# Second block: first convolution in three fp32r passes with low parts on GpSimd, and a new order of taps, inversion, z tiles and gate tiles

## The chip, the cores and the metric

One NeuronCore of a Trainium2 chip runs the whole program in one launch. The metric is the device time in microseconds of one execution; the inputs lie in device memory when it starts. TensorE is PE in the profile, VectorE is DVE, ScalarE is ACT, GpSimd is POOL, and SyncE (SP) issues most DMAs.

## The reference

All values are float32. The reference runs two networks, one behind the other, on 256 tokens of width 1024. The first (two layers of attention with Fourier mixing) fills the first 2058 us and is not touched. The second block is touched, in its mixer:

```python
hn = rmsnorm(h_res, norm_mix_g) * (1.0 + sc1) + sh1
proj = hn @ w_in        # a_qkv, a_z, a_gates, b_qk, b_v, b_o, b_gates, merge
a_qkv = silu(centred_conv(a_qkv, gdn_conv_w))      # 1536 channels, five taps along the tokens
aq, ak, av = split(a_qkv, 3)                        # q and k are normalised per head
o_a = gated delta rule of (aq, ak, av, g, beta), both directions, in chunks of 64
o_a = rmsnorm(o_a, gdn_norm_g) * silu(a_z)
b_qk = silu(centred_conv(b_qk, mlstm_conv_w))      # 1024 channels, five taps
h_b = mLSTM of (bq, bk, b_v, gates), both directions, in chunks of 64
h_b = head_layernorm(h_b) * sigmoid(b_o)
y = sigmoid(merge_a) * (o_a @ w_branch_a) + sigmoid(merge_b) * (h_b @ w_branch_b)
h_res = h_res + gt1 * (y @ w_out)
```

In each chunk the delta rule solves a unit lower triangular system of 64 rows. After the mixer comes a mixture of 32 experts (two per token, chosen in one of four groups), whose weights are some 100 MB, and a last norm.

## The kernel before

Activations lie transposed: a tile has 128 channels on the partitions and 256 tokens along the free axis. A projection tile is eight matmuls (k = 0 to 7, 128 rows of weights each) into one of seven PSUM banks, which a ring gives out in order of use. Engines run lists of instructions written out by hand (`pe_second`, `act_second`, `dve_second`, `pool_second`); there is no scheduler. An engine executes its list in order, and `e.wait_ge(*at(...))` waits for a named event of another engine, or of its own. Python generators mix two lists in fixed turns: each `yield` is a place at which the other list may get a turn.

A matmul of two fp32 operands takes several passes inside the array. The other form, `products` with `three` (L353), splits each operand into a high part (a copy to the fp32r type, by ACT) and a low part (the operand less the high part, by DVE, L539 and L1976) and makes three fp32r matmuls: high x low, low x high, high x high.

The second mixer, in the order of PE:

1. Norm of the input into U (eight tiles, L1080 on DVE, L1067 on ACT), then two gate tiles (L2259).
2. Twelve tiles of the first convolution ("gdn": four of k, four of q, four of v), fp32 x fp32 (L2038). For each, ACT copies the bank into one of three padded tiles `xp` (L2058), DVE multiplies by the first tap (L2065) and adds four more taps (L2070). ACT takes SiLU and squares of pairs of tiles (L2081, L2087). After the sixth tile PE makes the head sums (L2097) and turns k to tokens (L554), for which it waits for the squares of the first four tiles. The last two tiles are mixed into step 3.
3. Blocks: for each of eight heads, decays (L2156, L2143) and products of k with k (L2340), exponentials on ACT (L2352), 32x32 blocks on DVE (L2365).
4. Chunks: for each head, two decays and four products (L2433, L2434) in three banks, eight exponentials on ACT, two multiplications on DVE (L2447). The four z tiles (`pe_tile`, L2664) stand behind heads 1 to 4. DVE mixes in the inversion of the 32x32 blocks (`dve_invert`, L2381 and L2386: 62 short dependent steps, then two transposes, L2388 and L2389), the last convolution tile, and four right-hand sides (`dve_rhs`, L2466). The inverse is then copied into place (L2403 on ACT, L2411 on DVE).
5. Four tiles of the second convolution ("mlstm"), then the solve (`pe_solve`, L2477, L2488, L2504, L2509), with four more tiles of that convolution as filler.
6. The scan over chunks (L2607, L2622) beside the projections of v and the output gate (L2687, L2664) and DVE's gate rows of the mLSTM (`dve_gates_b`).
7. `pe_gdn_out`: the output of four pairs of heads, each with its norm. The "gate b" tiles, in three passes, are mixed in (`pe_gate_b`, L545): tile 0 ahead of the wait for the scan, tile f+1 in turn f, tiles 5 to 7 in the mLSTM loop (`pe_mlstm`) at heads 1, 3 and 5. Their high parts are made by ACT (L1970), their low parts by DVE (L1976).
8. The mLSTM, the "gate a" tiles and branches, the output projection, the router and the experts. The SP queue issues the experts' loads (L3651) in a fixed order, each when its place is free; before the first it waits for the last output of the mLSTM.

Weights come in loads of 2 MB into four slots `wr`. `late_low` names the same memory as the slots with the fp32r type: a low part takes the place of its raw weights. POOL has little to do in this block: two memsets for the unit matrix (L2574, L2576), one of the inverse's place (L2578), and at the end the indirect loads of some experts.

## Time and profile before

| | us |
|---|---|
| median of 3 runs | 2684.06 |
| lowest, highest | 2683.41, 2684.50 |
| profiled execution | 2682.79 |
| its span | 2681.0 |
| PE, DVE, ACT, POOL busy | 2600.6, 1634.2, 1002.4, 66.9 |
| granted TensorE clock, mean | 0.988 |

The span runs from the first to the last instruction of the profiled execution. Busy shares are averages over stages with different limits, so the stretches below are to be read one by one. The profile's matmul of fp32 operands is recorded as two instructions. A wait is put down to the event that came last.

### The profile page before, as it was taken

The numbers are of one execution on the slowest core, as the hardware profiler recorded it, in microseconds if no ns is written. First come the engines' busy times: TensorE is split into PE (matmuls) and PEld (weight loads), VectorE is DVE, ScalarE is ACT, GpSimd is POOL, SyncE is SP. The second block draws the span as 40 slices with busy tenths as digits, with TensorE's granted clock in tenths as the row PEclk, the third lists the DMA queues.
The fourth block names the chain that finished last, engine by engine and source line by source line (L and its number), as shares of the span: only waits on it lengthen the run. The fifth ranks groups of instructions, "written<-read, shape, count | busy, mean of one in ns | idle before, by whom it ended". The sixth has DMA issues, their size and how long they took to land.

```text
span 2681.0 us, 37410 instructions
## 1 busy us (share of the span) xinstructions
PE 2600.6 (97%) x15326; PEld 2148.8 (80%) x15326; DVE 1634.2 (61%) x2906; ACT 1002.4 (37%) x1777; POOL 66.9 (2%) x91
## 2 busy tenths in 40 slices
PE   8999999999999999999999999998999999999896
PEld 5888888867889888888888898798999787886453
DVE  4867766366446877648767465765555777675221
ACT  5322233266434322234222243664444442543121
POOL 0000000000000000000000000000000000000320
PEclk9999999999999999999999999999999999999998
DMA  7535442200222445434467433134345202149997
GB/s 320 198 155 225 179 182 95 95 32 32 77 112 95 175 178 220 165 126 157 174 250 281 158 123 132 43 134 181 139 180 192 95 32 95 64 172 418 412 395 322
DMA packets 48841, 456.55 MB, mean 170 GB/s; under 512 B 10784, under 2 KB 11168, under 8 KB 13344
## 3 DMA queue, kind: packets, MB, share of 16 engines
q1 hardware_dynamic: 41472, 446.01, 42.9%
q0 software_dynamic: 6912, 6.32, 0.7%
q8 instruction: 122, 2.00, 0.3%
q10 hardware_dynamic: 288, 1.84, 0.2%
q14 instruction: 47, 0.39, 0.0%
HBM read 497.11 MB, written 1.05 MB: 186 GB/s over the span
## 4 chain that ended last, share of the span: by engine, by line
PE 86%; DVE 7%; ACT 3%; DMA 3%; issue 2%; SPq 0%; POOL 0%; ACTq 0%; DVEq 0%; POOLq 0%
PE ps L545 68%; PE ps L3917 2%; PE ps L2038 2%; PE ps L1427 1%; PE ps L1450 1%; DMA BIG<-edn 1%; PE ps L554 1%; DMA BIG<-eup,extra_ids 1%; PE ps L3943 1%; PE nb L3943 1%; ACT fh L532 1%; DMA wr<-ws 1%; PE ps L3957 1%; PE ps L2664 1%; DVE fl L539 1%
## 5 line engine op out<-in xcount | busy, mean ns | idle before, releaser
L539 DVE TENSOR_TENSOR fl<-wr,fh 128x1024 fp32r<-128x1024 f32 (+2 forms) x436 | 481.9, 1107 | 446.0 <-ACT fh L532 445.2
L545 PE MATMUL ps<-UL,fh 128*128 128x512 f32 (+1 forms) x2096 | 731.9, 349 | 11.5 <-DVE UL L894 5.3
L545 PE MATMUL ps<-UH,fl 128*128 128x512 f32 (+1 forms) x2096 | 729.5, 348 | 0.0
L545 PE MATMUL ps<-UH,fh 128*128 128x512 f32 (+1 forms) x2096 | 729.1, 348 | 0.0
L532 ACT CAST fh<-wr 128x1024 fp32r<-128x1024 f32 (+2 forms) x436 | 414.4, 954 | 321.0 <-PE ps L545 298.8
L545 PEld LDWEIGHTS ps<-UL,fh 128*128 128x128 f32 x2096 | 397.7, 190 | 65.5 <-DVE UL L894 6.0
L545 PEld LDWEIGHTS ps<-UH,fh 128*128 128x128 f32 x2096 | 397.9, 190 | 49.8
L545 PEld LDWEIGHTS ps<-UH,fl 128*128 128x128 f32 x2096 | 397.7, 190 | 49.5
L597 DVE SCALAR_TENSOR_TENSOR acc<-wr,CA 128x1024 f32<-128x1024 f32 x256 | 312.4, 1220 | 3.7
L545 PE MATMUL ps<-HL,fh 128*128 128x512 f32 (+1 forms) x770 | 267.4, 347 | 0.0
L545 PE MATMUL ps<-HH,fl 128*128 128x512 f32 (+1 forms) x770 | 266.9, 347 | 0.0
L545 PE MATMUL ps<-HH,fh 128*128 128x512 f32 (+1 forms) x770 | 266.9, 347 | 0.0
L1247 ACT CAST HH<-rot 128x512 fp32r<-128x512 f32 (+1 forms) x88 | 50.0, 568 | 344.0 <-DVE rot L1290 344.0
L545 PEld LDWEIGHTS ps<-HL,fh 128*128 128x128 f32 x770 | 145.8, 189 | 18.3
L545 PEld LDWEIGHTS ps<-HH,fl 128*128 128x128 f32 x770 | 145.8, 189 | 18.1
L545 PEld LDWEIGHTS ps<-HH,fh 128*128 128x128 f32 x770 | 145.8, 189 | 18.0
L1290 DVE TENSOR_TENSOR rot<-ps,rot 128x512 f32<-128x512 f32 (+1 forms) x88 | 54.9, 623 | 137.7 <-PE ps L545 137.7
L1241 ACT ACTIVATE rot<-ps 128x512 f32<-128x512 f32 (+1 forms) x88 | 47.9, 545 | 203.3 <-PE ps L545 203.0
L3917 PE MATMUL ps<-wr,BIG 128*32 128x512 f32 x344 | 78.6, 613 | 1.5 <-DMA wr<-eup,extra_ids 1.5
L2038 PE MATMUL ps<-U,wr 128*128 128x256 f32 x320 | 74.0, 386 | 0.0
L3917 PE MATMUL ps<-BIG 128*32 128x512 f32 x284 | 71.4, 615 | 0.1
L2038 PEld LDWEIGHTS ps<-U,wr 128*128 128x128 f32 x320 | 60.4, 193 | 8.8 <-issue 0.4
(624 smaller groups left out, 3833.2 us busy)
## 6 DMA issues: line engine op xcount, KB each, us to landing
wr<-ws SPq DMA_DIRECT2D x135, 2048.0 KB, 8.1
wr<-ws SPq DMA_DIRECT2D x32, 1408.0 KB, 6.1
wr<-eup SPq DMA_DIRECT2D x27, 1024.0 KB, 17.3
BIG<-eup SPq DMA_DIRECT2D x26, 1024.0 KB, 14.2
wr<-edn SPq DMA_DIRECT2D x12, 1024.0 KB, 11.2
wr<-ws SPq DMA_DIRECT2D x11, 1024.0 KB, 6.9
BIG<-edn SPq DMA_DIRECT2D x11, 1024.0 KB, 10.0
X<-eup SPq DMA_DIRECT2D x6, 1024.0 KB, 11.6
```

Source lines behind the costliest of these rows:

```text
L532: e.copy(sp.tiles(n)[0], raw_tile(sp.units[n])).then_inc(*hi_done.inc("high", event))
L539: e.tensor_tensor(lv, raw_tile(sp.units[n]), hv.bitcast(F32), ALU.subtract).then_inc(*low_done.inc("low", event))
L545: i = e.matmul(out, l, r, start=first and n == 0, stop=last and n == len(pairs) - 1, skip_group_check=True)
L554: return e.transpose(out, in_, CC[0:k, 0:k])
L597: e.scalar_tensor_tensor(out=ACC[:, :], in0=w[:, q, :], scalar=1.0, in1=cb_rows[c], op0=ALU.mult, op1=ALU.mult, accum_out=to).then_inc(*mo ...
L1241: e.activation(s[:, 0:T], psum.of("gated", name, half, p, 0)[:, 0:T], ACT.Silu).then_inc(*act.inc("gated", name, half, p, 0))
L1247: e.copy(HH[:, p, 0:T], s[:, 0:T]).then_inc(*act.inc("h high", name, half, p))
L1290: e.tensor_tensor(s[:, 0:T], psum.of("gated", name, half, p, 1)[:, 0:T], s[:, 0:T], ALU.mult).then_inc(*dve.inc("gated", name, half, p, 1))
L1427: e.matmul(b[:, 0:khi - klo], qT[64 * c:64 * c + 64, h, q0:q0 + 128], kT[64 * c:64 * c + 64, h, klo:khi], start=True, stop=True, skip_grou ...
L2038: i = e.matmul(b[:, 0:256], w[:, k, q * 128:q * 128 + 128], U[:, k, 0:256], start=k == 0, stop=k == 7, skip_group_check=True)
L3917: i = e.matmul(b[o:o + 32, :], XG[(p // 2) % 2][:, k, 128 * (p % 2) + o:128 * (p % 2) + o + 32], up_weights(n, h, k % 4), start=k == 0, st ...
L3943: i = e.matmul(b[o:o + 32, :], actT[p % 2][:, q, o:o + 32], down_weights(n, q, h), start=q == 0, stop=q == 1, skip_group_check=True)
```

## The change

- The twelve tiles of the first convolution are made in three fp32r passes. ACT makes a high and DVE a low part of U (`act_conv_u`, `dve_conv_u`: two instructions of 128x1024 each). ACT makes the high part of each weight tile, in four rotating sets; POOL makes the low parts (`pool_conv_lows`), ahead of its memsets.
- In both convolutions ACT applies the middle tap while it reads the PSUM bank (a second instruction beside its copy), and DVE adds the other four. The first of DVE's five instructions goes.
- Inversion: its steps are spread over DVE's list 2, 4, 2, 7 to a place where they were 2 and, late, 5; the last two of the four early right-hand sides move into `dve_solve`.
- z tiles: behind heads 1, 3, 5 and 7; ACT copies them at heads 2, 4 and 6 and after the loop.
- Gate tiles: "gate b" tiles 0 and 1 stand ahead of the wait for the scan, tile f+2 in turn f, tiles 6 and 7 at heads 1 and 3 of the mLSTM. DVE makes the end blocks of the mLSTM in turn 1 of `dve_gdn_out`.

```diff
@@ -378,6 +378,7 @@
 
         columns_in = tally("columns_in")
         router_in = tally("router_in")
+        pool_low = tally("pool_low_parts")
         ident_in = tally("ident_in")
         x_in = tally("x_in")
         rope_in = tally("rope_in")
@@ -1863,6 +1864,7 @@
         ktok = big(1024, 2, 512)
         vtok = big(2048, 2, 1024)
         zf = big(1024, 4, 256)
+        intra_at = off[0]
         intra = big(4096, 8, 512)
         cross_at = off[0]
         CROSS = big(4096, 8, 512)
@@ -1975,6 +1977,38 @@
             e.wait_ge(*at("high", u))
             e.tensor_tensor(l, late_tile(weights(late_load(u)), u), h.bitcast(F32), ALU.subtract).then_inc(*low_done.inc("low", u))
 
+        CUH, CUL = [over(n, 4096 + cross_at + 2048 * i, [128, 8, 256]) for i, n in enumerate(("CUH", "CUL"))]
+        conv_sets = [over(f"ch{i}", 4096 + intra_at + 1024 * i, [128, 1024]) for i in range(4)]
+
+        def conv_parts(n):
+            n, load, q, wn, dst = conv_tiles("gdn")[n]
+            cols = slice(128 * q, 128 * q + 128)
+            raw, low = [t.rearrange("p (k n) -> p k n", k=8)[:, :, cols] for t in (weights(load), late_low[slot_of[load]][:, :])]
+            return load, raw, conv_sets[n % 4][:, :].rearrange("p (k n) -> p k n", k=8), low
+
+        def act_conv_high(e, n):
+            load, raw, high, low = conv_parts(n)
+            e.wait_ge(*at("loaded", load))
+            if n >= 4:
+                e.wait_ge(*at("conv proj", "gdn", n - 4))
+            e.copy(high, raw).then_inc(*hi_done.inc("high", "conv", n))
+
+        def pool_conv_lows(e):
+            for n in range(12):
+                load, raw, high, low = conv_parts(n)
+                e.wait_ge(*at("high", "conv", n))
+                e.tensor_tensor(low, raw, high.bitcast(F32), ALU.subtract).then_inc(*pool_low.inc("low", "conv", n))
+
+        def act_conv_u(e):
+            for i in range(2):
+                e.copy(CUH[:, 4 * i:4 * i + 4, :], U[:, 4 * i:4 * i + 4, 0:256]).then_inc(*act.inc("conv u high", i))
+
+        def dve_conv_u(e):
+            for i in range(2):
+                s = slice(4 * i, 4 * i + 4)
+                e.wait_ge(*at("conv u high", i))
+                e.tensor_tensor(CUL[:, s, :], U[:, s, 0:256], CUH[:, s, :].bitcast(F32), ALU.subtract).then_inc(*dve.inc("conv u", i))
+
         def act_late_u(e):
             e.wait_ge(*at("slot free", ("win2", 2080, 512)))
             for i in range(2):
@@ -2032,11 +2066,19 @@
             b, old = psum.take("conv in", tag, n)
             if old:
                 e.wait_ge(*at(*old))
-            if q == 0:
+            if tag == "gdn":
+                load, raw, high, low = conv_parts(n)
+                if n == 0:
+                    e.wait_ge(*at("conv u", 1))
+                e.wait_ge(*at("low", "conv", n))
+            elif q == 0:
                 e.wait_ge(*at("loaded", load))
             for k in range(8):
-                i = e.matmul(b[:, 0:256], w[:, k, q * 128:q * 128 + 128], U[:, k, 0:256], start=k == 0, stop=k == 7,
-                             skip_group_check=True)
+                if tag == "gdn":
+                    i = products(e, b[:, 0:256], three(high[:, k, :], low[:, k, :], CUH[:, k, :], CUL[:, k, :]), k == 0, k == 7)
+                else:
+                    i = e.matmul(b[:, 0:256], w[:, k, q * 128:q * 128 + 128], U[:, k, 0:256], start=k == 0, stop=k == 7,
+                                 skip_group_check=True)
                 if k % 2 and k < 7:
                     yield
             i.then_inc(*sums.inc("conv proj", tag, n))
@@ -2055,18 +2097,22 @@
             if (tag, n) == ("gdn", 0):
                 e.wait_ge(*at("conv edges"))
             e.wait_ge(*at("conv proj", tag, n))
-            e.copy(xp[:, 2:258], psum.of("conv in", tag, n)[:, 0:256]).then_inc(*act.inc("conv in", tag, n))
+            n, load, q, wn, dst = conv_tiles(tag)[n]
+            b = psum.of("conv in", tag, n)
+            e.copy(xp[:, 2:258], b[:, 0:256]).then_inc(*act.inc())
+            e.activation(dst, b[:, 0:256], ACT.Identity, scale=col("cva" if tag == "gdn" else "cvb", wn * 5 + 2, 1)).then_inc(
+                *act.inc("conv in", tag, n))
 
         def dve_conv(e, tag, n):
             n, load, q, wn, dst = conv_tiles(tag)[n]
             ck = "cva" if tag == "gdn" else "cvb"
             xp = xps.of("conv taps", tag, n)
             e.wait_ge(*at("conv in", tag, n))
-            e.tensor_scalar(dst, xp[:, 0:256], col(ck, wn * 5, 1), None, ALU.mult).then_inc(*dve.inc())
-            for i in range(1, 5):
-                before = dve.now()
-                yield
-                e.wait_ge(*before)
+            for i in (0, 1, 3, 4):
+                if i:
+                    before = dve.now()
+                    yield
+                    e.wait_ge(*before)
                 e.scalar_tensor_tensor(out=dst, in0=xp[:, i:i + 256], scalar=col(ck, wn * 5 + i, 1), in1=dst,
                                        op0=ALU.mult, op1=ALU.add).then_inc(*dve.inc())
             dve.mark("conv taps", tag, n)
@@ -2553,6 +2599,7 @@
                                      *[itertools.chain(dve_conv(e, "mlstm", n), dve_first_block_out(e, col("fin"), n - 4))
                                        for n in range(4, 8)])
             for n in range(2):
+                dve_rhs(e, 2 + n)
                 for _ in dve_conv(e, "mlstm", n):
                     pass
             for n in range(8):
@@ -2877,8 +2924,8 @@
                 pe_chunks(e, h)
                 if h == 6:
                     pe_to_tokens(e, "v a", zf, ("conv silu", 11))
-                if 1 <= h <= 4:
-                    pe_tile(e, "z", h - 1, ("win2", 1536, 512), h - 1, h == 4)
+                if h % 2:
+                    pe_tile(e, "z", h // 2, ("win2", 1536, 512), h // 2, h == 7)
             for n in range(4):
                 pe_conv(e, "mlstm", n)
             pe_solve(e)
@@ -2889,6 +2936,9 @@
 
         def act_second(e, prev):
             act_norm_pair(e, "nmix", prev, m2[:, 0])
+            act_conv_u(e)
+            for n in range(2):
+                act_conv_high(e, n)
             act_log_exp(e)
             e.activation(st[0:64, 8:9], a_log, ACT.Exp).then_inc(*act.inc("a log"))
             act_softplus(e, "a", NX)
@@ -2896,8 +2946,10 @@
             for to, src in ((NEGR, CA[:, 0:256]), (CROSSR, CA[:, 256:512]), (ROWR, CA[:, 512:576]), (IDR, ident)):
                 e.copy(to[:, :], src).then_inc(*act.inc())
             act.mark("consts2 parts")
+            act_conv_high(e, 2)
             for n in range(9):
                 act_conv(e, "gdn", n)
+                act_conv_high(e, n + 3)
                 if n == 8:
                     e.wait_ge(*at("C"))
                     act_row_high(e, "B", RHB, BC)
@@ -2927,17 +2979,21 @@
                     act_row_high(e, "E", RHE, EA)
                 if h in (2, 5):
                     act_conv(e, "gdn", 10 + (h - 2) // 3)
+            def act_z(q):
+                e.wait_ge(*at("z proj", q))
+                e.copy(z_raw[:, q, :], psum.of("z", q)[:, 0:256]).then_inc(*act.inc("z", q))
+
             for h in range(8):
                 act_chunks(e, h)
                 if h == 6:
                     act_to_tokens(e, "v a", vtok)
-                if 2 <= h <= 5:
-                    e.wait_ge(*at("z proj", h - 2))
-                    e.copy(z_raw[:, h - 2, :], psum.of("z", h - 2)[:, 0:256]).then_inc(*act.inc("z", h - 2))
+                if h in (2, 4, 6):
+                    act_z(h // 2 - 1)
                 if h == 3:
                     for n in (8, 10):
                         act_silu_square(e, n)
                     act_log_exp(e)
+            act_z(3)
             e.wait_ge(*at("products sum", 7))
             e.wait_ge(*act.now())
             e.activation(zs, z_raw, ACT.Silu).then_inc(*act.inc("z open"))
@@ -2965,6 +3021,8 @@
             e.memset(eps64, 64 * EPS).then_inc(*dve.inc())
             dve.mark("conv edges")
             dve_norm_pair(e, "nmix", col("fin"), col("nmix"), m2[:, 1])
+            e.wait_ge(*at("u", "nmix", 7))
+            dve_conv_u(e)
             gates = dve_gdn_gates(e)
             next(gates)
             e.wait_ge(*at("gate sum", 1))
@@ -2989,7 +3047,7 @@
                 dve_blocks(e, h)
                 if h == 1:
                     dve_end_blocks(e, "gdn", ends)
-                for _ in range((0, 0, 0, 0, 1, 1, 1, 2)[h]):
+                for _ in range((0, 0, 0, 0, 1, 1, 1, 1)[h]):
                     next(taps)
                 if h == 4:
                     dve_row_low(e, "A", RHA, AR)
@@ -3000,7 +3058,7 @@
                                            op1=ALU.add).then_inc(*dve.inc("A"))
             invert = dve_invert(e)
             for n, _ in enumerate(dve_beside(e)):
-                for _ in range(2 if n < 14 else 5):
+                for _ in range(2 if n < 5 or 7 <= n < 11 else 4 if n < 7 else 7):
                     next(invert, None)
             for _ in invert:
                 pass
@@ -3024,12 +3082,13 @@
                 if h == 1:
                     yield from dve_conv(e, "gdn", 11)
             e.wait_ge(*at("tokens", "v a", 1))
-            for h in range(4):
+            for h in range(2):
                 dve_rhs(e, h)
                 yield
 
         def pe_gdn_out(e):
             pe_gate_b(e, 0)
+            pe_gate_b(e, 1)
             e.wait_ge(*at("scan a"))
             for f in range(4):
                 b, old = psum.take("o square", f)
@@ -3052,7 +3111,7 @@
                             i = e.matmul(b[pp, 64 * n:64 * n + 64], SP[pp, s, o:o + 64], qg[pp, 2 * f + dr, 64 * n:64 * n + 64],
                                          start=False, stop=True, skip_group_check=True)
                 i.then_inc(*sums.inc("o", f))
-                pe_gate_b(e, f + 1)
+                pe_gate_b(e, f + 2)
                 b, old = psum.take("o root", f)
                 if old:
                     e.wait_ge(*at(*old))
@@ -3065,6 +3124,7 @@
 
         def act_gdn_out(e):
             act_gate_b(e, 0)
+            act_gate_b(e, 1)
             for f in range(4):
                 r, old = heads_rot.take("gdn out", f)
                 if old:
@@ -3077,7 +3137,7 @@
                 e.activation(r[:, 256:512], psum.of("o root", f)[:, 0:256], ACT.Ln, scale=1.0 / 64, bias=eps[:, :]).then_inc(*act.inc())
                 e.wait_ge(*act.now())
                 e.activation(r[:, 256:512], r[:, 256:512], ACT.Exp, scale=-0.5).then_inc(*act.inc("o root", f))
-                act_gate_b(e, f + 1)
+                act_gate_b(e, f + 2)
                 act_late_high(e, 4 + f)
                 if f:
                     act_oa_high(e, f - 1)
@@ -3097,6 +3157,8 @@
                     e.wait_ge(*at("z open"))
                 e.tensor_tensor(oaT[:, f, :], oaT[:, f, :], zs[:, f, :], ALU.mult).then_inc(*dve.inc("gdn out", f))
                 dve_late_low(e, 3 + f)
+                if f == 1:
+                    dve_end_blocks(e, "mlstm", MP[:, 20:24])
                 if f > 1:
                     dve_oa_low(e, f - 2)
 
@@ -3126,8 +3188,8 @@
                     tk = slice(tt * 128, tt * 128 + 128)
                     i = e.matmul(b[:, tk], kb[pp, f, tk], qb[pp, f, tk], start=True, stop=True, skip_group_check=True)
                 i.then_inc(*sums.inc("kq", "mlstm", h))
-                if h in (1, 3, 5):
-                    pe_gate_b(e, 5 + h // 2)
+                if h in (1, 3):
+                    pe_gate_b(e, 6 + h // 2)
             for s in range(3):
                 for dr in range(2):
                     n, tt, pb = chunk_of(s, dr)
@@ -3221,8 +3283,8 @@
                         e.activation(r[:, o:o + 128], b[:, o:o + 128], ACT.Exp,
                                      bias=CTB[:, tt, 0, 32 * dr + h:32 * dr + h + 1]).then_inc(*act.inc())
                 act.mark("exp decay", "mlstm", h)
-                if h in (1, 3, 5):
-                    act_gate_b(e, 5 + h // 2)
+                if h in (1, 3):
+                    act_gate_b(e, 6 + h // 2)
                 if h % 2:
                     act_late_high(e, 8 + h // 2)
             e.wait_ge(*act.now())
@@ -3282,7 +3344,6 @@
             dve_late_low(e, 7)
             dve_oa_low(e, 2)
             dve_oa_low(e, 3)
-            dve_end_blocks(e, "mlstm", MP[:, 20:24])
             e.wait_ge(*at("cols", "mlstm", 1))
             for _ in dve_pairs(e, "qi", qg, qb):
                 pass
@@ -4181,6 +4242,7 @@
         def _(e):
             for l in range(2):
                 pool_mirror(e, l)
+            pool_conv_lows(e)
             pool_second(e)
             pool_expert_loads(e)
```

## Rows read from the trace of the kernel before

**Rows 1.** Busy by stretch: us, PE, PEld, DVE, ACT, POOL (counts), clock, DMA share, GB/s
```profile
2070.50:2109.50 39.00, 38.23 (x181) 32.27 (x180) 27.07 (x67) 15.79 (x27) 0.00 (x0) 1.00 0.43 162
2109.50:2131.00 21.50, 20.94 (x109) 16.57 (x110) 15.57 (x41) 13.27 (x44) 0.00 (x0) 1.00 0.18 59
2131.00:2188.50 57.50, 51.15 (x249) 43.32 (x247) 46.66 (x114) 29.88 (x82) 3.51 (x1) 0.91 0.14 52
...
2304.00:2330.00 26.00, 26.00 (x181) 23.13 (x182) 14.69 (x25) 15.46 (x41) 0.00 (x0) 0.87 0.21 81
...
2391.00:2681.00 290.00, 253.60 (x1974) 144.68 (x1974) 93.04 (x239) 66.68 (x135) 48.05 (x48) 0.96 0.96 389
```

**Rows 2.** Timeline of SP's queue, first expert load: start, us, engine, line, operation
```profile
2391.84 0.45 SPq L3651 DMA_DIRECT2D wr<-eup  x1
```

**Rows 3.** Chain of waits: start, us, what; six tiles now, then three-pass products
```profile
2070.65 20.73 PE ps L2038 x96
...
2379.42 4.31 PE ps L545 x36
```

**Rows 4.** Timeline of ACT, a copy of a tile and a high part of weights
```profile
2091.46 0.37 ACT L2058 COPY BIG<-ps 128x256 f32<-128x256 f32 x1 [3.08 <-PE ps L2038]
...
2283.23 1.05 ACT L1970 CAST lh<-wr 128x1024 fp32r<-128x1024 f32 x1
```

**Rows 5.** Timeline of DVE: first tap, four taps, a low part of weights
```profile
2091.87 0.35 DVE L2065 TENSOR_SCALAR BIG<-BIG,K 128x256 f32<-128x256 f32 x1 [1.02 <-ACT BIG L2058]
2092.26 2.04 DVE L2070 SCALAR_TENSOR_TENSOR BIG<-BIG,K 128x256 f32<-128x256 f32 x4
...
2283.97 1.22 DVE L1976 TENSOR_TENSOR late<-wr,lh 128x1024 fp32r<-128x1024 f32 x1
```

**Rows 6.** Timeline of POOL: copy and subtraction alone, then one beside DVE
```profile
573.05 0.19 POOL L1726 COPY acc<-rot 128x2 f32<-128x2 f32 x1 [8.91 <-ACT rot L1666]
573.19 0.45 POOL L1727 TENSOR_TENSOR acc<-rot 128x127 f32<-128x127 f32 x1
...
629.39 0.91 POOL L1727 TENSOR_TENSOR CA<-rot 128x127 f32<-128x127 f32 x1
```

**Rows 7.** Timeline of DVE at the same place
```profile
629.31 1.55 DVE L1798 TENSOR_TENSOR FL<-acc,FH 128x512 fp32r<-128x512 f32 x2
630.78 0.94 DVE L1798 TENSOR_TENSOR FL<-RS,FH 128x512 fp32r<-128x512 f32 x1
631.85 0.69 DVE L1798 TENSOR_TENSOR FL<-CA,FH 128x512 fp32r<-128x512 f32 x1
```

**Rows 8.** Timeline of DVE in the chunks, a wait
```profile
2159.89 0.69 DVE L2447 TENSOR_TENSOR BIG<-ps,BIG 128x512 f32<-128x512 f32 x1 [3.78 <-ACT BIG L2352]
```

**Rows 9.** Timeline of PE: mLSTM tiles, first and second products of the solve
```profile
2170.40 14.08 PE L2038 MATMUL ps<-U,wr 128*128 128x256 f32 x64
2188.57 1.63 PE L2477 MATMUL ps<-acc,BIG 128*128 128x128 f32 x8 [4.09 <-issue]
...
2192.94 1.05 PE L2477 MATMUL ps<-acc,BIG 128*128 128x128 f32 x8
```

**Rows 10.** Timeline of ACT, the inverse copied into place
```profile
2182.85 3.29 ACT L2403 COPY BIG<-BIG 32x512 f32<-32x512 f32 x3 [1.35 <-DVE BIG L2388]
```

**Rows 11.** Timeline of PE, outputs of the first two pairs of heads
```profile
2274.37 1.98 PE L3042 MATMUL ps<-BIG 128*64 128x128 f32 x16 [2.16 <-DVE BIG L2835]
...
2282.05 1.09 PE L3042 MATMUL ps<-BIG 128*64 128x128 f32 x16
```

**Rows 12.** Timeline of ACT, root of a norm in pe_gdn_out's second turn
```profile
2287.52 0.47 ACT L3077 ACTIVATE rot<-ps,eps 128x256 f32<-128x256 f32 x1 [2.51 <-PE ps L3060]
```

**Rows 13.** Timeline of DVE: second turn, first wait of the mLSTM loop, its last low part
```profile
2288.48 0.48 DVE L3093 SCALAR_TENSOR_TENSOR BIG<-BIG,K,rot 128x256 f32<-128x256 f32 x1 [3.29 <-ACT rot L3079]
...
2315.12 0.69 DVE L3296 TENSOR_TENSOR BIG<-ps,rot 128x512 f32<-128x512 f32 x1 [4.99 <-PE ps L3127]
...
2328.41 1.21 DVE L1976 TENSOR_TENSOR late<-wr,lh 128x1024 fp32r<-128x1024 f32 x1
```

## Prediction

> **What bounds the kernel now.** I read the stages first, as busy time by stretch [rows 1]: from 2070.5 us on, PE is busy 38.23 of 39.00 us while twelve convolution tiles begin, then 20.94 of 21.50, then 51.15 of 57.50. Over the last 290 us the DMA engines are 0.96 busy: the experts' weights set the end there. Their first issue is at 2391.84 us [rows 2], and it stands behind the last mLSTM output. So what the second block gains or loses before 2391.84 moves the whole DMA-bound tail with it, microsecond for microsecond, and none of it is hidden. The question is when the last mLSTM output comes. Then I followed the chain of waits and, where it names PE, asked who is next behind. I take four stretches, A to D.
>
> **A: the twelve tiles in three passes (2070.5 to 2131 us).** Six tiles of four-pass fp32 take 20.73 us, 3.455 each; 36 fp32r passes of the same width take 4.31, so 24 take 2.87 [rows 3]. PE saves 12 x 0.58 = 7.0 us.
>
> The price is on three engines. ACT makes 12 high parts at 1.05 and 12 first taps about as long as its 0.37 copy [rows 4]: 17 us more beside its 15.79 + 13.27 of 60.5 [rows 1], bearable, but in series with its copies. DVE gains: a tile's first tap (0.35) goes, 2.04 for four taps stays [rows 5]; it pays two low parts of U, 1.22 each [rows 5]. POOL makes 12 low parts. The trace has no such instruction of 1024 elements. A 128x127 one took 0.45 and a 128x2 copy 0.19 [rows 6]: (0.45 - 0.19) x 1024/127 + 0.19 = 2.3 us. Scaling the whole 0.45 gives 3.6; from below stands DVE's 1.22 for the same subtraction [rows 5]. I take 2.3, worked out on its own engine, and under PE's 2.9: POOL alone doesn't pace the tiles.
>
> What decides is POOL beside DVE. At 629.39 us the 0.45 us instruction took 0.91, while DVE ran subtractions with both inputs in SBUF [rows 6]. DVE's three took 2.41 (629.31 to 631.72) where one alone takes 0.69 [rows 7]: at least 0.34 lost to the two POOL reads of 0.26 each. POOL's extra 0.46 is more than its own reading time of 0.26 (0.45 less the 0.19 of start), which two engines sharing each cycle fairly couldn't make of it; waiting for a whole DVE instruction can. So I read an exclusive turn per instruction, and four taps (all with two SBUF inputs) meet it. DVE then loses some 2.1 us per low part, less 0.1 of start-up: 2.04 + 2.0 = 4.05 us per tile, against 3.455 now. That row is one of 127 elements; that it holds through a 2.3 us instruction is my extrapolation.
>
> What the row can't show, the length of the turn for long instructions, the Trainium skill states, and it speaks against this change ("SBUF — State Buffer", section Who interferes with whom): a VectorE instruction with two SBUF inputs and a GpSimd one that reads SBUF exclude each other, and the later one is blocked until the first has finished, however long that is. By this rule a low part of any length blocks DVE for all of it and the sum is the forecast's; by the row taken alone (turns no longer than 0.26 us shown) it would be rival 1's.
>
> Stepping it through: the U parts end on ACT at 2069.2 and on DVE at 2070.6; the first low part is there at 2072.8, so PE starts 2.2 us late and, as after its 2.16 us gap in [rows 11], runs slow for some 3 us, at the lower of the two clocks, 1.2 GHz (1.5 lost). ACT issues high part n+3 as soon as copy n is out, which may be up to three tiles ahead of DVE (three xp buffers), so POOL runs to low part 8 while DVE is at tile 3. By the time that tile 3 has its taps, DVE and POOL have spent 9 x 2.1 = 19 us of POOL's reading, 4 x 2.04 = 8.2 of taps and some 4 of gate rows (busy 27.07 in the stretch [rows 1], less nine tiles of 2.4 and the row parts), in the 31.4 us since 2070.6: the turns are the bound. Tile 3 ends near 2102; the squares, the head sums and the tokens of k wait for it, and PE takes tile 6 at about 2105, 10 us later than now. After that come tiles 6 to 8, three low parts (6.3), gate rows and tap work of 10, less what PE's shorter tiles give. DVE starts its blocks 14 us later; the blocks themselves shift whole. A = +14. The two memsets of the unit matrix now stand behind the low parts on POOL's queue, near 2120; the inversion that waits for them starts at 2135 or later, so they cost nothing, and lose this cover only if POOL runs 15 us over. The loads that wait for the slots of these tiles come later by as much as the tiles; DMA is 0.43 and 0.18 busy there [rows 1], and no wait for them is due. Bounds: with low parts of 1.22 us the count gives 12 x 1.1 less, +1; if the turns cost nothing, ACT's longer series leaves +1.5 (PE's 7.0 are eaten by the late start, the clock, and ACT's squares and table loads between longer tiles); with 3.6 us low parts the same count gives 12 x 1.3 = 16 more, +30.
>
> **B: inversion, chunks, z tiles (2131 to 2188.5).** DVE waits 3.78 us, and 3.2 once more, for products held up behind z tiles [rows 8]. With a z tile after every second chunk and the inversion's 62 steps packed 4 and 7 to a place, they end right behind chunk 7, before the right-hand sides, of which two move behind the inversion. DVE is through its copies some 8 us earlier. But PE stands behind: its four mLSTM tiles run 14.08 us from 2170.40 and end at 2184.5, and the solve starts at 2188.57 after 4.09 idle [rows 9]. Only that gap can go. ACT's third mLSTM copy still waits for its tile (PE at 2181.1, three of the four), and 3.29 us of inverse copies follow it [rows 10], so the solve starts near 2185.3: -3.3. The gap also cost clock: the first eight products took 1.63 against 1.05 afterwards [rows 9], 0.6, and the tile steps behind them, twice the work, some 1.3 (an estimate from that). B = -5.2, between -2 (DVE's longer chunk spacing stalls PE) and -8.
>
> **C: solve.** The two moved right-hand sides lie in DVE's wait for the first cross products; a first tap less per tile shortens its end. -0.5, between +1 and -1.5.
>
> **D: gates (2274 to 2330).** Gate tile 1 goes ahead of the wait for the scan, where PE idles 2.16 us and then runs slow (1.98 against 1.09 for the same sixteen) [rows 11]. The cost: tile f+2 now needs the low part that DVE makes in turn f-1. From PE's norm: 0.96 to DVE's start (ACT from 2287.52, DVE from 2288.48), 0.48 and a second like it (0.4), then 1.22 = 3.1 us [rows 5, 12, 13]; PE has only the outputs of 1.9 to do meanwhile, so 1.2 us of stall in each of three turns, +4 at the last norm. In the mLSTM loop, PE then has two gate tiles where it had three, and DVE, which waited 4.99 us there for PE, becomes the pace: loop and low parts end near 2325.6 in place of 2329.6 [rows 13]. The end blocks' instruction moves under a wait, worth nothing more. D = -4.0, between 0 (the stalls bring the lower clock) and -6.
>
> **Sum.** +14 - 5.2 - 0.5 - 4.0 = +4.3 on the profiled execution's own 2682.79 us (span 2681.0 and 1.8 around it) is 2687.1; the median of the runs is 1.3 above that execution, so 2688.4.
>
> **Rivals.**
> 1. *POOL's reads don't hold DVE up* (the 629 us row was something else, or a long instruction lets DVE in between). For it: only short instructions were seen. Against: both engines' lengthenings there match. A = +1.5 to +5; total 1.5 - 9.7 = -8 to -5: 2676 to 2679. DVE's taps stay near 0.51 apart.
> 2. *Lock and lower clock together*, the slower side: PE's gaps of 7 us in A and of 1.2 us in D each bring the clock of 1.2 GHz, as the gap of 4.09 did [rows 9]. Three drops at 1.7 us beyond those counted, and D at 0: +4.3 + 5 + 4 = +13, 2697. It decides once PE waits over about 2 us at three more places. For: stretch 2304 to 2330 is at 0.87 already [rows 1]. Against: DVE, not PE, would be the bound in A, and hides PE's slowness there.
> 3. *Low parts as slow as 3.6 us*: total +20, 2704. Against it: the fixed 0.19 is seen in the copy.
>
> **How the numbers follow.** A comparison of this kernel can tell about 0.2%, 5.4 us, from no change. Lock as forecast: 0.56, spread 4 to each side: same 0.34, slower 0.20, faster 0.02. Rival 1: 0.34, faster 0.30, same 0.04. Rivals 2 and 3: 0.10, slower. Together faster 0.32, same 0.38, slower 0.30. Likeliest's own range 2683 to 2694; with both sides 2674 to 2698.
>
> **What would show it.** Right: DVE's tap instructions in A with many of 2 us and more, beginning beside POOL subtractions; POOL's at 2.2 to 2.5; tile 6 on PE at about 2105; PE idle 15 us in all between 2070 and 2125; the solve without a gap before it; three waits of PE for the low parts of gates; first expert issue near 2396. Wrong: taps at 0.48 throughout, and tiles on PE 2.9 apart (rival 1); granted clock under 0.9 in A and D (rival 2). If POOL's instruction is shorter than 1.9 us, A falls by 12 x 0.4 and the sum to zero.

## The result

The changed kernel takes 2700.56 us in the median of six runs (2694.63 to 2704.63), against 2683.90 for six of the kernel before; the ratio is 1.006 [1.005, 1.0069]. The forecast was 2688.4 with 2674 to 2698: the direction was right, the size was not. The profiled execution took 2703.9 us (span 2702.1, granted clock 0.984); it is the second slowest of the six.

I read both traces at the same six places and take differences of differences, so what the first block leaves as run-to-run offset drops out (the second block's first U part is at 2061.94 in the trace of before and at 2065.05 after; nothing ahead of it was changed).

| stretch, by its last event | forecast | measured |
|---|---|---|
| A: to DVE's first inversion transpose | +14 | +18.0 |
| B: to the start of the solve on PE | -3.3 (and -1.9 of clock behind it) | -2.7 |
| C, and D to ACT's last norm | -0.5 + 4 | +6.4 |
| D: mLSTM loop, to DVE's memset | -8 | -3.5 |
| tail, to the first expert load | 0 | 0.0 |

With the +3.1 of offset the sum is the +21.3 of the first expert load, which answers to [rows 2]:

```profile
2413.13 0.44 SPq L3712 DMA_DIRECT2D wr<-eup  x1
```

Busy time by stretch of the changed kernel (time, PE, PEld, DVE, ACT, POOL, granted clock, DMA share, GB/s), beside [rows 1]: in the first, PE is busy 25.88 of 39.00 us where it was busy 38.23, at a granted clock of 0.82 where it was 1.00; POOL is new with 21.84; no engine is full. The last row is the mLSTM loop.

```profile
2073.60:2112.60 39.00, 25.88 (x177) 23.82 (x177) 30.45 (x42) 21.31 (x37) 21.84 (x9) 0.82 0.28 108
2112.60:2155.00 42.40, 32.86 (x217) 28.36 (x215) 32.31 (x64) 26.05 (x68) 10.77 (x6) 0.96 0.27 100
2155.00:2207.00 52.00, 50.30 (x244) 42.75 (x243) 47.38 (x114) 29.96 (x81) 1.21 (x1) 0.90 0.11 41
2323.07:2351.07 28.00, 26.41 (x183) 22.90 (x182) 19.11 (x32) 18.87 (x50) 0.00 (x0) 0.88 0.20 76
```

POOL's low parts in the same trace (start, us, engine, line): all twelve take 2.34 to 2.70 us, 2.44 in the median, where 2.3 was forecast, but with idle time between them that ends with ACT's high part. Three of the rows:

```profile
2079.05 2.38 POOL L2000 TENSOR_TENSOR late<-wr,ch 128x1024 fp32r<-128x1024 f32 x1 [0.63 <-ACT ch L1994]
2097.44 4.64 POOL L2000 TENSOR_TENSOR late<-wr,ch 128x1024 fp32r<-128x1024 f32 x2 [3.77 <-ACT ch L1994]
2115.69 2.40 POOL L2000 TENSOR_TENSOR late<-wr,ch 128x1024 fp32r<-128x1024 f32 x1 [13.61 <-ACT ch L1994]
```

DVE there. Four taps take 2.04 where POOL stands still (2095.07 to 2097.11) and 4.18 or 6.19 beside it; eight scans take 5.93, where they took 1.68 before (the same line then L2242). A blocked instruction is longer by up to 2.2 us, most of a low part: the chain of waits has single taps of 0.50 and of 2.63, and the gate row of L2270 takes 2.63 for 0.42 (before: L2224).

```profile
2081.51 4.18 DVE L2116 SCALAR_TENSOR_TENSOR BIG<-BIG,K 128x256 f32<-128x256 f32 x4 [4.43 <-ACT BIG L2103]
2085.61 2.63 DVE L2270 SCALAR_TENSOR_TENSOR BIG<-BIG 128x256 f32<-128x256 f32 x1
2088.28 6.19 DVE L2116 SCALAR_TENSOR_TENSOR BIG<-BIG,K 128x256 f32<-128x256 f32 x4
2095.07 2.04 DVE L2116 SCALAR_TENSOR_TENSOR BIG<-BIG,K 128x256 f32<-128x256 f32 x4
2097.15 5.93 DVE L2288 TENSOR_TENSOR_SCAN BIG<-BIG 32x64 f32<-32x64 f32 x8
2103.49 5.96 DVE L2116 SCALAR_TENSOR_TENSOR BIG<-BIG,K 128x256 f32<-128x256 f32 x12
```

PE's waits in the changed kernel, where they matter: the late start, the long gap ahead of the head sums, and behind it tile 6 (A); the solve's start, a gap inside it and its last products (B, C); low parts of gate tiles (D).

```profile
2076.04 0.36 PE L546 MATMUL ps<-CUL,ch 128*128 128x256 f32 x1 [2.28 <-POOL late L2000]
2106.92 1.97 PE L2143 MATMUL ps<-rot,CA 128*64 128x256 f32 x4 [9.94 <-ACT rot L2133]
2110.44 0.56 PE L546 MATMUL ps<-CUL,ch 128*128 128x256 f32 x1
2206.97 1.16 PE L2523 MATMUL ps<-acc,BIG 128*128 128x128 f32 x8 [0.60 <-ACT BIG L2449]
2244.07 1.97 PE L2550 MATMUL ps<-acc,BIG 128*128 128x64 f32 x16 [1.73 <-DVE acc L2608]
2250.93 1.91 PE L2555 MATMUL ps<-BIG,rot 128*64 128x128 f32 x16
2298.80 0.36 PE L546 MATMUL ps<-UGL,lh 128*128 128x256 f32 x1 [1.49 <-DVE late L1978]
2305.97 0.36 PE L546 MATMUL ps<-UGL,lh 128*128 128x256 f32 x1 [1.35 <-DVE late L1978]
```

### The profile page after: what moved, and what is told of

Same layout as the page of the kernel before. It is cut to its first block, busy times and chain, and to the rows that moved or that the text cites. A ratio compares the mean times of both kernels' runs of the same rounds, so it can differ in the third digit from the quotient of the medians.

```text
span 2702.1 us, 37648 instructions
## 1 busy us (share of the span) xinstructions
PE 2602.7 (96%) x15422; PEld 2151.9 (80%) x15422; DVE 1649.4 (61%) x2888; ACT 1022.8 (38%) x1811; POOL 96.5 (4%) x103
## 3 DMA queue, kind: packets, MB, share of 16 engines
q8 instruction: 123, 2.02, 0.3%
## 4 chain that ended last, share of the span: by engine, by line
PE 83%; DVE 8%; ACT 4%; DMA 3%; issue 2%; POOL 0%; SPq 0%; ACTq 0%; DVEq 0%; POOLq 0%
PE ps L546 68%; PE ps L3978 2%; PE ps L1451 1%; PE ps L1428 1%; DMA BIG<-edn 1%; PE ps L555 1%; DVE BIG L2116 1%; ACT fh L533 1%; DMA BIG<-eup 1%; PE ps L4004 1%; DMA wr<-eup,extra_ids 1%; PE ps L4018 1%; DVE fl L540 1%; PE nb L4004 1%; PE ps L2734 1%
## 5 line engine op out<-in xcount | busy, mean ns | idle before, releaser
L1242 ACT ACTIVATE rot<-ps 128x512 f32<-128x512 f32 (+1 forms) x88 | 47.9, 545 | 203.3 <-PE ps L546 203.0
L1615 ACT ACTIVATE BIG<-ps,st 128x512 f32<-128x512 f32 (+1 forms) x96 | 58.0, 620 | 21.4 <-DVE st L1785 21.2
L1785 DVE TENSOR_REDUCE st<-ps 128x1 f32<-128x512 f32 (+1 forms) x96 | 50.9, 592 | 24.2 <-PE ps L1428 24.2
```

What stands on the lines that cost most here:

```text
L1242: e.activation(s[:, 0:T], psum.of("gated", name, half, p, 0)[:, 0:T], ACT.Silu).then_inc(*act.inc("gated", name, half, p, 0))
L1615: e.activation(dst[:, 0:nk], psum.of("p", l, n, qb, c)[:, 0:nk], ACT.Exp, bias=st[:, z + c:z + 1 + c], scale=-1.0, accum_out=st[:, z + 4 + ...
L1785: e.tensor_reduce(st[:, z + c:z + c + 1], psum.of("p", l, n, qb, c)[:, 0:nk], AX.X, ALU.min).then_inc(*dve.inc("least", l, n, qb, c))
```

## The experiments

The theory was the forecast's: POOL's subtractions and DVE's instructions with two SBUF inputs take turns at SBUF, each for a whole instruction. Rivals for A were a longer series on ACT, the late start, and sharing by bytes; for D, the lower clock against the waits for low parts. The stretches below are differences from the trace of before, as in the table above (A | B | C and D to the last norm | loop):

| kernel | median us | ratio | A | B | C, D | loop |
|---|---|---|---|---|---|---|
| changed | 2700.6 | 1.0060 [1.0050, 1.0069] | +18.0 | -2.7 | +6.4 | -3.5 |
| split_only | 2701.9 | 1.0067 [1.0053, 1.0081] | +19.3 | -1.0 | -0.3 | 0.0 |
| no_split | 2681.2 | 0.9994 [0.9984, 1.0005] | +0.3 | -2.8 | +4.8 | -6.5 |
| dve_lows | 2684.3 | 1.0001 [0.9992, 1.0010] | +8.6 | -3.0 | +4.8 | -4.2 |
| pool_memset | 2684.4 | 1.0000 [0.9991, 1.0009] | -1.8 | -2.9 | +4.8 | -4.1 |
| pool_copy | 2683.6 | 0.9990 [0.9981, 1.0000] | +3.2 | -2.6 | +6.4 | -3.5 |
| pool_eighths | 2690.8 | 1.0025 [1.0014, 1.0036] | +15.5 | -3.2 | +4.8 | -4.2 |
| eighths_apart | 2692.8 | 1.0029 [1.0018, 1.0040] | +10.8 | -2.9 | +4.7 | -4.1 |
| inv_taps | 2685.1 | 1.0003 [0.9994, 1.0012] | +0.4 | -2.9 | +0.3 | +1.5 |
| gates_only | 2685.2 | 1.0004 [0.9995, 1.0013] | 0.0 | -0.1 | +4.4 | -3.5 |
| early_lows | 2677.2 | 0.9978 [0.9969, 0.9987] | +0.4 | -2.8 | +0.6 | -4.2 |
| early_four | 2676.5 | 0.9968 [0.9956, 0.9980] | +0.3 | -2.8 | -1.4 | -2.7 |
| early_four_gate6 | 2674.8 | 0.9967 [0.9955, 0.9979] | +0.4 | -2.9 | -1.4 | -6.9 |

A profile is one execution; the medians are over 5 to 11, and one kernel's runs lie up to 13 us apart (no_split: 2677.2 at a mean clock of 0.989 to 2690.1 at 0.986). Stretches are what I compare; totals only where the intervals part. A stretch stands for its one execution, and that isn't always a typical one: the profile of dve_lows (2688.1) is the slowest of its eleven runs, that of pool_memset (2678.9) the fastest of its eleven, that of pool_eighths (2696.4) the slowest of its seven. So dve_lows and pool_memset lie 10.4 us apart in A and 0.1 us apart in the median.

**Which part costs.** split_only is the kernel before with the three-pass tiles alone.

```diff
+            pool_conv_lows(e)        # and the tiles in three passes, U parts, high parts
             pool_second(e)           # taps, inversion, z tiles, gates: as before
```

> The kernel before with only the three-pass tiles (U parts, high parts by ACT, low parts by GpSimd); taps, inversion, z tiles and gates as before. Theory (GpSimd subtractions and DVE instructions with two SBUF inputs take exclusive turns, one instruction at a time): the tiles cost about what the changed kernel shows in that stretch, +17 us, so 2698 to 2704, with taps of 4.18 us for two beside the subtractions. Rival (the stretch is long because the changed taps and ACT's longer series hold it up, not the parts): under +8 us, below 2692. Rival (the other three edits together gain nothing): equal to the changed kernel, 2700.6.

It came out at 2701.93, with the taps lengthened as in the changed kernel (0.77 us in the mean). That is the theory's range and also the last rival's number: the total alone can't tell them apart. no_split is the reverse.

```diff
-                    i = products(e, b[:, 0:256], three(high[:, k, :], low[:, k, :], ...
+                    i = e.matmul(b[:, 0:256], w[:, k, q * 128:q * 128 + 128], U[:, k, 0:256], ...
```

> The changed kernel without its three-pass tiles: fp32 tiles in four passes again, no parts of U and none of the weights; the taps, the inversion, the z tiles and the gates as changed. Theory (from the stretches of the changed kernel: B -2.7, C +1.1, D +0.9 with the stalls of 1.2 us in the gates): -1 to -3 us against before, 2681 to 2683. My forecast's terms B, C and D (-5.2, -0.5, -4.0) would give -9.7, 2674. Rival (the stalls and the losses in C and D come from GpSimd's late work or from the shifted loads of the three-pass tiles): -6 us or more, below 2678.

2681.22, in the theory's range: the three passes cost 19 us, all of the loss and more, and the rest, forecast at -9.7, gives 3.3, with an interval that holds no change.

**What of the three passes costs.** dve_lows moves the twelve low parts to DVE, pool_memset takes POOL's reads away, pool_copy leaves it one input.

```diff
-            pool_conv_lows(e)
+                dve_conv_low(e, n + 3)      # dve_lows: behind the taps of tile n
---
-                e.tensor_tensor(low, raw, high.bitcast(F32), ALU.subtract)...
+                e.memset(low.bitcast(F32), 0.0)...      # pool_memset, twice
+                e.tensor_copy(low, raw)...              # pool_copy
```

> The changed kernel, but the twelve low parts are made by DVE (1.2 us each, 14.6 us more of DVE work) and GpSimd makes none. Theory of exclusive turns: DVE gets back about 12 x 2.1 us of blocked time and pays 12 x 1.2, so the first stretch costs some 8 us less than in the changed kernel: 2689 to 2694. Rival (no exclusion; the two engines share, so work moved onto the busier DVE costs its full 14.6 us, less what GpSimd's late parts cost PE): not under 2700, up to 2710.

> The changed kernel, but in place of each low part of the first convolution's weights GpSimd sets the same 1024 columns to zero, twice: the low parts are left out of the products, all instructions of the other engines stay. GpSimd is about as busy and writes more, but it reads nothing. Theory (its reads are what shuts DVE out): DVE's taps at 0.5 us, the first stretch at +2 to +5 instead of +17: 2685 to 2690. Rival (GpSimd's writes or its semaphores hold DVE up as well): taps stay above 1 us each and the time above 2697.

> The changed kernel, but GpSimd copies the weight's 1024 columns in place of subtracting (one input from SBUF instead of two; the low parts are left out of the products, a copy stands in their place). If any GpSimd read takes the port for its whole instruction, DVE's taps beside it last 1 us and more, in step with the copy's length (about 1.2 to 1.5 us), and the first stretch costs +5 to +12: 2689 to 2697. If only GpSimd instructions with two inputs do, the taps stay at 0.48 and the time is that of the memsets, 2684.

dve_lows gives DVE 12 x 1.22 us more to do and still ends A 9.4 us sooner; its median, 16 us below the changed kernel's, is better than the 2689 to 2694 that I expected. In pool_memset all the other instructions stand, POOL is busy 2 x 0.954 per tile (a low part took 2.44), and A is 19.8 us shorter than in the changed kernel: at -1.8, and 2684.4 in the median, it lies under the +2 to +5 and the 2685 to 2690 that I expected. Its groups in 2068 to 2130, DVE's taps and scans, POOL's memsets, and one more of DVE's (last: busy, mean ns):

```profile
L2118 DVE SCALAR_TENSOR_TENSOR BIG<-BIG,K 128x256 f32<-128x256 f32 x42 | 20.2, 485 | 14.1 <-ACT BIG L2105 12.9
L2290 DVE TENSOR_TENSOR_SCAN BIG<-BIG 32x64 f32<-32x64 f32 x8 | 1.7, 260 | 0.1
L2002 POOL MEMSET late<- 128x1024 f32 x12 | 11.4, 954 | 0.7
L2346 DVE TENSOR_SCALAR BIG<-BIG,st 64x256 f32<-64x256 f32 x1 | 1.0, 1033 | 0.0
```

So ACT's longer series and a start of PE 1.52 us late cost nothing here; with POOL's reads gone the cost is gone. Two things went with them. The long gap ahead of the head sums shrank to 2.02 us, and PE's clock in 2068 to 2130 was 1.00, against 0.89 in the changed kernel: how much of A the lower clock cost beside DVE's waits, this run doesn't separate. dve_lows, at 0.89 too but with taps of 0.485, is 9.4 us shorter in A, so the clock isn't the whole of it. And the last row of the four doesn't fit "reads" alone: an instruction with one SBUF input took 1.03 us beside a memset, and 0.34 before (L2298). pool_copy's time was far below my 2689 to 2697, and its A, +3.2, below my +5 to +12, but its taps do wait: beside copies of 1.16 they last up to 1.24, which is 0.76 longer and less than a whole copy. In the two traces A is 5.0 us longer than with the memsets; the medians of the two kernels don't differ.

```profile
L2116 DVE SCALAR_TENSOR_TENSOR BIG<-BIG,K x42: 471/485/1244, 2075.5 to 2131.7; 128x256 f32<-128x256 f32 x42
L2000 POOL CAST late<-wr 128x1024 fp32r<-128x1024 f32 x12 | 13.9, 1163 | 352.5 <-ACT ch L1994 352.5
```

**Turns or bytes.** The same bytes in eight instructions per low part, back to back and then each behind the last one's end:

```diff
-                e.tensor_tensor(low, raw, high.bitcast(F32), ALU.subtract)...
+                for k in range(8):
+                    e.tensor_tensor(low[:, k, :], raw[:, k, :], high[:, k, :].bitcast(F32), ALU.subtract)...
+                    e.wait_ge(*pool_low.now())      # eighths_apart only
```

> The changed kernel, each low part made by GpSimd in eight subtractions of 128 columns (about 0.45 us each alone) in place of one of 1024. Theory (DVE is shut out for one GpSimd instruction at a time, and GpSimd for one of DVE): taps of 0.6 to 0.9 us, none of 1.2 or more in the mean of a tile, and DVE ready earlier, while GpSimd needs 3.6 us and up per low part and now paces the tiles: 2695 to 2710. Rival (DVE is slowed by the bytes that GpSimd reads, however they are cut): taps of 1 to 2 us in the mean as in the changed kernel, and a time further up by GpSimd's own longer work.

> As the kernel with the low parts in eight subtractions each, but GpSimd waits for the end of each before it issues the next. With the eight back to back one tap of DVE lasted 11.50 us (2081.23 to 2092.73), over 24 GpSimd subtractions. Theory (DVE gets its turn only when GpSimd's next instruction isn't at the port already): with a pause after each subtraction no tap lasts over 1.5 us. Total 2688 to 2698, since GpSimd itself is slower. Rival (the long tap came from something else, or whoever has the port keeps it): a tap of several us again.

Both are 8 to 10 us faster than the changed kernel although POOL now works 46 to 48 us in place of 30; pool_eighths is even under the 2695 to 2710 that I expected. The same bytes lengthened the taps by 10.2 us in sum in the changed kernel (28.6 us for 38, at 0.485 each alone) and by 3.5 us in eighths_apart (22.9 for 40), so it isn't bytes. But the half of the theory that said "one POOL instruction at a time" fell: back to back, a single tap lasted 11.50 us, while POOL ran 48 subtractions at 0.43 each without a pause; the tap ended 0.27 us after the last of them. Apart, no tap passed 0.743. What is left of A there (+10.8) goes with POOL's own pace, 47.9 us of work for twelve tiles: DVE waits 19.9 us for tiles. First pool_eighths (DVE, then POOL), then the taps of eighths_apart (ns: least, median, most).

```profile
2081.23 11.50 DVE L2118 SCALAR_TENSOR_TENSOR BIG<-BIG,K 128x256 f32<-128x256 f32 x1 [6.97 <-ACT BIG L2105]
2071.85 20.61 POOL L2001 TENSOR_TENSOR late<-wr,ch 128x128 fp32r<-128x128 f32 x48 [328.25 <-ACT ch L1994]
2104.21 6.68 DVE L2118 SCALAR_TENSOR_TENSOR BIG<-BIG,K 128x256 f32<-128x256 f32 x12
```

```profile
L2119 DVE SCALAR_TENSOR_TENSOR BIG<-BIG,K x40: 485/566/743, 2080.8 to 2124.3; 128x256 f32<-128x256 f32 x40
```

The third row is from the same kernel, beside POOL's next series: there the taps pass at 0.56 each. Why it alternates there and not at 2081 stays open, and so does whether the long tap comes in every execution: this one is the slowest of the seven. The two totals are within each other's intervals.

**The other edits.** inv_taps and gates_only do one half each of no_split: the kernel before with one group of the edits. One line of each:

```diff
+            for _ in range(2 if n < 5 or 7 <= n < 11 else 4 if n < 7 else 7):   # inv_taps
+                pe_gate_b(e, f + 2)                                             # gates_only
```

> The kernel before with only the changed taps, inversion, z tiles and right-hand sides; fp32 tiles in four passes and the gates as before. Theory (the stretches add; those of the kernel without the three passes gave A +0.3, B -2.8, C 0): -2 to -3 us, 2681 to 2683. My forecast (B -5.2, C -0.5) would give 2678 to 2679.

> The kernel before with only the changed gates (gate tile 1 ahead of the scan, two tiles instead of three in the mLSTM loop, end blocks in the second turn). Theory (stalls of 1.2 us in three turns, +4 at the last norm, given back in the mLSTM loop but for what the lower clock there takes): -2 to +1 us, 2682 to 2685.5. My forecast had -4.0, 2680.5.

inv_taps: its profiled execution, 2681.86, lies in the theory's range and its median, 2685.13, does not; gates_only's 2685.21 lies in its range, 2682 to 2685.5. Neither half can be told from no change. The trace of inv_taps shows what held C up: tile 7's taps are drawn ahead of the solve's sixth subtraction, DVE waits 5.02 us there for ACT's copy, and PE waits behind it.

```profile
2220.17 1.01 DVE L2108 SCALAR_TENSOR_TENSOR BIG<-BIG,K 128x256 f32<-128x256 f32 x2 [5.02 <-ACT BIG L2095]
2221.92 1.97 PE L2542 MATMUL ps<-acc,BIG 128*128 128x64 f32 x16 [1.73 <-DVE acc L2600]
```

early_lows is no_split with DVE's late low parts a turn earlier; early_four also draws four steps to a turn instead of five; the last also moves gate tile 6 ahead of the loop and tile 7 behind its head 2.

```diff
+            dve_late_low(e, 3)                       # early_lows
-                dve_late_low(e, 3 + f)
+                dve_late_low(e, 4 + f)
-                for _ in range(5):                   # early_four
+                for _ in range(4):
+            pe_gate_b(e, 6)                          # early_four_gate6
             pe_pairs(e, "qi", PICKB, RH4, "b4")
```

> The changed kernel without its three-pass tiles, and with each of DVE's late low parts (3 to 7) one turn earlier, so that the gate tile of a turn never waits for a low part made in that turn. Theory (the low part made in turn f-1 is what PE waits for): period of the norms back at 5.4 us from 6.75, last norm 3 to 4 us earlier than without this, total 2677 to 2679. Rival (the period is long because ACT or PE itself carries the gate tile's work there): period still over 6.5 us, total 2681.

> The kernel with the early low parts (no three-pass tiles), and DVE's work beside the solve in four steps to a turn instead of five. Theory: since the taps have one step less, five steps a turn bring tile 7's taps ahead of the sixth subtraction of the solve; DVE waits 5.02 us for ACT there and PE 1.73 us for DVE. With four steps that wait goes, and the total falls by 1.7 to 2 us against 2677.2: 2675.3. Rival (PE waits there for ACT's copy or the tile in any case): no change, 2677.

> As the one with four steps, and gate tile 6 ahead of the mLSTM's row products, where PE idles 0.84 and some 1 us more, with tile 7 behind head 2. Theory (in the mLSTM loop PE is the pace, and the loop costs 25.0 us at the full clock and 27.4 to 28 at the lower one, which it falls to when PE's work thins out ahead of the heads): the clock stays up there more often, and the time falls by 1 to 3 us, 2672 to 2674. Rival (ACT's chain of the first heads is what PE waits for, and a gate tile ahead of it makes it late): 1 to 3 us slower than the one with four steps.

early_lows: the norms are 5.38 us apart again (ACT at 2291.29 and 2296.67; 6.75 without it), and 4 us of the median go, as expected; its interval and no_split's overlap a little, so the spacing is what shows it. early_four: the 1.73 wait is gone and its stretch is 2.0 shorter, -1.4 against +0.6; the median fell by 0.8 only, which is inside the scatter, and its profiled execution gave part back in the loop (-2.7). early_four_gate6, at 2674.8, lies just above its 2672 to 2674. The clock of the loop shows in the loop's rows of early_four (0.82), no_split (1.00), gates_only (0.88) and early_four_gate6 (1.00), in this order:

```profile
2295.83:2324.65 28.82, 27.82 (x183) 24.02 (x182) 18.06 (x31) 18.85 (x50) 0.00 (x0) 0.82 0.20 74
```

```profile
2300.83:2325.86 25.03, 23.43 (x183) 20.03 (x182) 19.11 (x32) 18.84 (x50) 0.00 (x0) 1.00 0.22 84
```

```profile
2304.05:2332.04 27.99, 26.39 (x183) 22.76 (x182) 19.12 (x33) 18.87 (x50) 0.00 (x0) 0.88 0.20 76
```

```profile
2296.25:2320.84 24.59, 23.01 (x183) 19.97 (x182) 18.24 (x32) 18.85 (x50) 0.00 (x0) 1.00 0.23 87
```

no_split and gates_only issue the same 183 matmuls there behind the same waits (0.84, 0.17, 0.6); one fell to 1.2 GHz at the second head (a matmul of 128x512 there took 0.80 for 0.50), the other stayed at 2.4. The loop is PE's, and the drop costs 3 us. inv_taps has the loop of the kernel before and took 1.5 us more for it, at 0.84 where the trace of before had 0.89: so much can come without any edit. Whether moving tile 6 prevents it, as its one profile suggests, one trace can't show; its median is 1.7 below early_four's, not apart from it. The three of this group beat both kernels: 0.2 to 0.3% under the one before.

## Why the prediction was wrong

Without the offset the trace lies 13.9 us over the forecast (+18.2 for +4.3). A is 4.0 of it, B's gap 0.6, C with the norms of D 4.8, the loop 4.5.

**The mechanism of A held, and the row that carried it was rightly read.** POOL's instruction, 2.34 to 2.70 against 2.3; taps beside it longer by most of a low part; PE's late start, 2.28 against 2.2, and the slow first tile behind it, 4.62 for 2.87 (1.5 forecast, 1.75 measured). Rivals 1 and 3 fell: pool_memset shows the taps at 0.485 throughout that rival 1 stood for, and no low part took 3.6. The length of the turn, which before the change only the Trainium skill gave ("SBUF — State Buffer", section Who interferes with whom: the later one is blocked until the first has finished), is now in the traces for a 2.4 us instruction (0.50 to 2.63); the 11.50 us tap beside a series of short ones is beyond that rule.

**That tile 3 ended near 2102 was partly luck.** Its taps end at 2105.5, less the offset 2102.4. The count that gave 2102 was 19 us of POOL's reading, 8.2 of taps and 4 of gate rows. DVE's rows over these 32 us add up otherwise: 14.3 of blocking (three taps, two gate rows and the scans), 8.2 of taps, 5.1 of gate rows, and 4.43 of waiting for the first tile's copy. Nine low parts were made, but some of them ran while DVE had nothing to do; the count had all nine block it and left its wait out, and the two errors are nearly equal.

**The step that failed in A is the term behind tile 3: PE "takes tile 6 at about 2105".** Tile 6 came at 2110.44 - 3.1 = 2107.3. Behind the 9.94 gap the head sums took 1.97, as slow as the 1.98 of [rows 11], and the tokens of k behind them 1.97 for 1.09, at a granted clock of 0.50 from 2106.9 to 2110.4; I had left the clock out there and put it down to rival 2. With the 0.4 of tile 3 that is 2.3 of the 4. The rest lies behind tile 6. "POOL runs to low part 8 while DVE is at tile 3" was true, but then POOL stood 13.61 us, since ACT makes high part 9 only behind copy 6, and low part 9 began at 2115.69. The last three held DVE up for what was forecast (6.3): 2.1 over four taps, 2.2 over a gate row, 1.9 over the next eight taps. But tile, low part, taps and blocks then followed one another without overlap, and the blocks began 17.2 late and ended 18.0 late; I had let the blocks shift by 14, whole.

**B** was right in its gap: 4.09 became 0.60, and the solve's first eight products take 1.16 for 1.63. In inv_taps the third group of products (PE at 2187.54; 2192.94 before) is 4.5 earlier, once 1.24 of offset and A's 0.35 are taken off; forecast 5.2. The table has the gap alone.

**C: "a first tap less per tile shortens its end" had the wrong sign.** A shorter tile makes a list drawn five steps at a time run ahead of its inputs. The 1.73 of PE's wait ate what the clock had given back: with the gates as before (inv_taps) the stretch is +0.3, where -0.5 and -1.9 of clock were forecast; without that wait, in early_four, it is 2.0 us shorter. In the changed kernel's execution PE also fell to 1.2 GHz near the solve's end (its last sixteen products took 1.91 at 2250.93; 1.09 before at 2232.20), and the stretch is 1.6 us longer than in no_split, which has the same waits of 1.73 and 0.87 ahead of these products and took 1.09; the trace of pool_copy has the same +6.4.

**D: the stalls were sized well (+4.4 for +4, early_lows takes them out), the sentence "DVE ... becomes the pace" was wrong.** DVE is busy 18 to 19 us of the loop in the traces of the changed gates, PE 23.0 to 27.8: PE is still the pace, with a tile less to do. -8 was to be had only nearly, and at the full clock (-6.5, -6.9); at a mean of 0.82 to 0.88 it is -2.7 to -4.2. The row with 0.87 in [rows 1] said that the drop was there already, and I should have counted on it staying.

**Rival 2 came with the likeliest, not in its place.** Its sign, a granted clock under 0.9 in A and D, is in the trace: 0.82 in A's first 39 us, 0.88 in the loop. Its price was 2697, and with rival 3 I gave it 0.10. On PE's path the slow clock is 1.8 us behind the 9.94 gap, 1.6 from the solve's end on and 3.0 in the loop (against no_split). The forecast put the clock at nothing in these three places, and they are 6.4 of the 13.9.

By medians: the three-pass tiles +19.3 (changed kernel less no_split) where A was to be +14, the rest -3.3 for -9.7. Each miss is small and all have one sign; the range had no term for misses that go together.

## What to carry to other kernels

Work given to an idle engine is not free of the busy one: where a trace shows that their instructions block each other, price what overlaps at the sum of their times, leave out what falls into a wait, and ask for the order in which the last ones fall. Where a list of steps is drawn at a fixed rate beside a chain, shortening its items moves its waits; re-read where each wait lands. Price a stretch at the granted clock that its row shows, not at the full one.

## What the runs showed of the hardware that I had not expected

- A single DVE tap of 0.48 us lasted 11.50 us while GpSimd ran some 26 subtractions of 0.43 back to back (seen once, in one execution); with each behind the end of the last, the longest tap was 0.743. One long GpSimd instruction (2.4) lengthens a DVE instruction by up to 2.2 us and then lets it in.
- It isn't only instructions with two full inputs: a GpSimd copy of 1.16 us lengthened taps to 1.24, and eight scans of 32x64 went from 1.68 to 5.93 in all beside subtractions. In split_only the first tap, with one SBUF input, took up to 2.39 for 0.35.
- Memsets of 0.95 left the taps alone (0.485, the most 0.488), but not every DVE instruction: beside one, a tensor_scalar of 64x256 with one SBUF input took 1.03 for 0.34, and two copies of 32x4 took 1.53 for 0.35.
- The same 183 matmuls behind the same waits ran at 1.00 in one execution and at 0.88 in another.
